# Two transformer blocks on one core: one ScalarE function set with logarithm and exponential, asked for by name ahead of each layer norm

## The reference

```
def layer_norm(x, g, b):
    xf = x.astype(jnp.float32)
    mu = jnp.mean(xf, axis=-1, keepdims=True)
    var = jnp.mean(jnp.square(xf - mu), axis=-1, keepdims=True)
    return ((xf - mu) * lax.rsqrt(var + EPS) * g + b).astype(x.dtype)

for l in range(DEPTH_2):                       # second block, l = 0, 1
    h = x * (1.0 + sc_m) + sh_m
    y = even_mixer(h, ...) if l % 2 == 0 else spatial_gating_mixer(h, ...)
    x = layer_norm_2(ALPHA * x + (1.0 + g_m) * y, ln_g[l, 0], ln_b[l, 0])
    h = x * (1.0 + sc_f) + sh_f
    y = swiglu(h, ...) if l % 2 == 0 else moe_swiglu(h, ...)
    x = layer_norm_2(ALPHA * x + (1.0 + g_f) * y, ln_g[l, 1], ln_b[l, 1])
```

## Time and profile before

| | us |
|---|---|
| median of 3 runs | 2342.64 |
| lowest, highest | 2341.39, 2345.26 |
| the profiled execution, its own time | 2345.24 |
| its span in the trace | 2343.4 |

### The profile page before, as it was taken

How to read it: one execution, slowest core, us unless ns; L and a number is a source line. 1 busy time by engine, 2 the same in 40 slices (tenths; PEclk the granted TensorE clock), 3 DMA queues, 4 the chain that set the end, 5 groups by cost and what they waited for, 6 DMA issues and landing times.

```text
span 2343.4 us, 25110 instructions
## 1 busy us (share of the span) xinstructions
PE 2232.7 (95%) x10088; PEld 1823.9 (78%) x10088; DVE 1600.0 (68%) x1938; ACT 1299.0 (55%) x1569; POOL 17.8 (1%) x16
## 2 busy tenths in 40 slices
PE   8999999997999989799989899999999999999997
PEld 7668877886888866678857788888888888888885
DVE  0266234535999953355422599999999999899994
ACT  1145113105777743344420477787777787778784
POOL 0000000000000000000000000000000000000000
PEclk9999999997999999999999799999999999999998
DMA  8465455755999972045350499999999998999992
GB/s 344 183 254 231 162 202 228 271 214 217 383 367 351 354 285 108 0 180 191 149 217 1 175 392 368 368 362 364 378 352 379 350 381 343 373 352 386 350 371 83
DMA packets 52991, 645.43 MB, mean 275 GB/s; under 512 B 8832, under 2 KB 10624, under 8 KB 14080
## 3 DMA queue, kind: packets, MB, share of 16 engines
q1 hardware_dynamic: 48320, 630.34, 69.6%
q10 hardware_dynamic: 3104, 8.13, 0.9%
q0 software_dynamic: 1440, 5.24, 0.6%
HBM read 640.55 MB, written 3.15 MB: 275 GB/s over the span
## 4 chain that ended last, share of the span: by engine, by line
PE 90%; DVE 4%; ACT 2%; issue 2%; DMA 1%; SPq 0%; ACTq 0%; DVEq 0%
PE psum L1755 56%; PE psum L1545 19%; PE psum L1537 5%; PE psum L1864 2%; DVE stage_lo L1343 1%; PE psum L1639 1%; PE psum L1777 1%; DMA ring<-w_branch_in 1%; PE psum L1650 1%; PE psum L1765 1%; ACT arena L569 1%; DVE h_lo L1440 0%; DMA ring<-w_in_in 0%; PE psum L1567 0%; PE psum L1486 0%
## 5 line engine op out<-in xcount | busy, mean ns | idle before, releaser
L1343 DVE TENSOR_TENSOR stage_lo<-ring,stage_hi 128x1024 fp32r<-128x1024 f32 (+1 forms) x934 | 1103.0, 1217 | 94.5 <-ACT stage_hi L962 77.7
L962 ACT ACTIVATE stage_hi<-ring 128x1024 fp32r<-128x1024 f32 (+1 forms) x934 | 964.4, 1055 | 305.7 <-PE psum L1755 227.4
L1755 PE MATMUL psum<-stage_hi,x_hi 128*128 128x512 f32 (+1 forms) x1344 | 530.2, 395 | 12.8 <-DVE x_lo L1372 8.8
L1755 PE MATMUL psum<-stage_hi,x_lo 128*128 128x512 f32 (+1 forms) x1344 | 522.2, 389 | 0.0
L1755 PE MATMUL psum<-stage_lo,x_hi 128*128 128x512 f32 (+1 forms) x1344 | 520.7, 387 | 0.0
L1755 PEld LDWEIGHTS psum<-stage_hi,x_hi 128*128 128x128 f32 x1344 | 253.2, 188 | 62.2 <-issue 9.1
L1755 PEld LDWEIGHTS psum<-stage_hi,x_lo 128*128 128x128 f32 x1344 | 253.1, 188 | 53.3
L1755 PEld LDWEIGHTS psum<-stage_lo,x_hi 128*128 128x128 f32 x1344 | 253.6, 189 | 49.3
L1755 PE MATMUL psum<-stage_hi,h_hi 128*128 128x512 f32 x664 | 260.1, 392 | 10.0 <-DVE h_lo L1440 9.8
L1755 PE MATMUL psum<-stage_lo,h_hi 128*128 128x512 f32 x664 | 258.5, 389 | 0.0
L1545 PE MATMUL psum<-arena,ring 128*128 128x256 f32 x1024 | 227.1, 382 | 5.6 <-ACT arena L569 3.8
(11 more groups left out here) (218 smaller groups left out, 1685.8 us busy)
## 6 DMA issues: line engine op xcount, KB each, us to landing
ring<-moe_w_gate_in SPq DMA_DIRECT2D x56, 2048.0 KB, 9.3
ring<-moe_w_up_in SPq DMA_DIRECT2D x56, 2048.0 KB, 9.4
ring<-moe_w_down_in SPq DMA_DIRECT2D x56, 2048.0 KB, 9.2
ring<-w_in SPq DMA_DIRECT2D x48, 2048.0 KB, 8.9
ring<-ada_w_in SPq DMA_DIRECT2D x15, 2048.0 KB, 8.0
ring<-w_in_in SPq DMA_DIRECT2D x14, 2048.0 KB, 10.7
mixer_tiles<-ada_w_in SPq DMA_DIRECT2D x9, 2048.0 KB, 7.8
mixer_tiles<-w_in_in SPq DMA_DIRECT2D x6, 2048.0 KB, 12.5
```

Source lines behind the costliest of these rows:

```text
L962: act.activation(chunk_view(stage_hi, f, side, p, c), chunk_source(f, side, p, c), ACT.Copy)\
L1343: dve.tensor_tensor(chunk_view(stage_lo, f, side, p, c), chunk_source(f, side, p, c), chunk_view(stage_hi, f, side, p, c).bitcast(F32), AL ...
L1755: ins = pe.matmul(dst, a, b, start=start, stop=stop)
```

## The change

A function `keep_ln_exp` on ScalarE asks for the set `natural_log_exp_and_others` by name. It is called in five places of ScalarE's program: behind the last Sigmoid of the first mixer, behind the last Gelu of the third mixer, and behind each of the three feed-forward stages. The second of those in the order of the program serves two layer norms, since between numbers 1 and 2 ScalarE uses no other function than Exp, Square, Copy and Identity. The arithmetic stays as written, with Exp now read from this set. Nothing is changed on the other engines.

```
+        def keep_ln_exp():
+
+            act.preload_act_table_set("natural_log_exp_and_others")
...
                         ins = act.activation(gate[:, 2 * i + k, :], bank(b, 2, T)[:, k, :], ACT.Sigmoid,
                                              bias=col_a("b_gate", n * KT + 2 * i + k))
                     ins.then_inc(bank_free[b], 1)
+                    if n == 2 and i == 3:
+                        keep_ln_exp()
...
                     if a == "od_u":
                         act.activation(mix[:, 2 * i:2 * i + 2, :], bank(b, 2, T), ACT.Gelu_apprx_tanh)\
                            .then_inc(bank_free[b], 1)
+                        if i == 3:
+                            keep_ln_exp()
...
             passes(act, n, feeds[n], unit, joined)
+            keep_ln_exp()
         walk(plans[3])
```

## The result

The changed kernel takes 2331.62 us (median of 5 runs, 2330.01 to 2332.82) against 2342.64 before. The ratio of the two is 0.9944 with a 95% interval of 0.9934 to 0.9955: 0.56% faster, where 7.6 us or 0.33% were forecast. The medians differ by 11.0 us, the ratio stands for 13.1. The second is nearer the truth: in the interleaved runs of the experiments the kernel before had medians of 2344.06 to 2345.13, above the 2342.64 of its first runs. Its profiled execution took 2331.94 us with a span of 2330.1.

A forecast was written before the change was run, and what follows sets the result against it. TensorE makes up 90% of the chain of waits, and ScalarE's loads matter only where it waits, in six layer norms. 6 x 1.27 = 7.6 us off 2342.64, all else 0, gave 2335.0 us, range 2331.0 to 2340.0.

The forecast's parts named there:

- The chain and the loads in it: Six layer norms: the load between logarithm and exponential delays TensorE; removing it gains 1.27 us each, 7.6 us (7.3 to 7.9).
- All six pass it on: Behind each layer norm's exponential: the whole gain reaches TensorE; tightest in layer norm 2, with 0.13 us to spare on VectorE.
- The removed load ahead of the logarithm at nothing: Six layer norms: this load runs under TensorE's sum with idle time behind it (2.45 us in number 0), gaining nothing.
- The added loads at nothing: Five earlier loads of 1.28 us on ScalarE: hidden in idle time of at least 6.77 us, costing nothing.
- The transfers behind the added load at 0: Ahead of layer norm 3: four transfers on ScalarE's queue behind the load cost 0, with 4.5 us as upper end.
- The sum: Whole kernel: -7.6 + 0 = -7.6 us, taken from the median of 2342.64 to give 2335.0.
- The forecast's own stretch: Whole kernel: 2332.5 to 2337.5 us around the forecast of 2335.0, given 60%.
- The same clock brings more: Rival on TensorE's clock: two more stretches at full clock give -7.6 - 3.4, 2331.6 us; chance 12%.
- The clock as the other side: Rival: sums of squares fall to half clock, 1.69 us each; 2338 to 2342 (8%), or 2343.5 and above (3%).
- a drain of 1.38 us: Rival at the six loads: a drain hidden in recorded durations goes too, gain 16.0 us, time 2326.6; chance 3%.
- late transfers: Rival ahead of layer norm 3: transfers behind the added load come late, 2339.5 us, or 2337 in half; chance 9%.
- hidden loads: Rival in the layer norms: loads are hidden anyway, or the set doesn't serve both functions; nothing gained, 2342.6 us; chance 5%.

The follow-up runs named there:

- every Copy put back: Changed kernel with a ScalarE Copy of 128x1280 between logarithm and exponential, in all six or some layer norms; in all six 2344.70 us, ratio to before 1.0000.
- Delays in four layer norms: Changed kernel with a ScalarE Copy of 1.27 us between logarithm and exponential in layer norms 0, 2, 4 and 5: 2343.64 us; in 1 and 3 alone: 2338.49.
- two added products in each pause: Changed kernel with two added products (0.9 us at full clock) on TensorE in each pause behind the sum of squares: 2335.14 us, ratio 0.9953.
- the Copy in layer norm 0: Changed kernel with a ScalarE Copy of 1.27 us between logarithm and exponential in layer norm 0 alone: 2336.56 us, ratio to before 0.9965.
- the reverse edit: Changed kernel with a ScalarE Copy of 128x1280 between logarithm and exponential in each layer norm: 2344.70 us, ratio to before 1.0000.

## Why the prediction was right or wrong

*The chain and the loads in it: right.* The load between the two functions was a link; the gap left is 0.03 us where 0.04 was taken, and the pauses are 1.28 us shorter where 1.27 was forecast. Six of them make 7.7 us for 7.6.

*All six pass it on: right.* VectorE in layer norm 2, the tightest place, takes up the exponential at once.

*The removed load ahead of the logarithm at nothing: right,* and shown alone (ratio 1.0002). *The added loads at nothing: right.* All five ran in idle time.

*The transfers behind the added load at 0: right.* All four were issued ahead of it and landed in time.

*The sum: wrong by its missing term.* The step that failed is "The saving is of fixed durations, so it holds for the median too". The sum has no term for TensorE's clock: it was put at nothing, with chances on both sides, since its falls vary. For the sum of squares in layer norm 0 that was so: it went both ways between the pairs of traces. Over the whole kernel it wasn't. With the shorter pauses the time at half clock went from 94 to 77 us on average, for every Copy put back it rose again, and the time moved with it. This term, at 0 in the sum, measured 11.0 - 7.7 = 3.3 us by the medians, 13.1 - 7.7 = 5.4 by the ratio, and 4.7 over all runs of both kernels, where 17 us less at half clock at 0.30 us each make 5.0. In the traces the largest parts are 2.1 us around layer norm 1 and 2.4 in the stages behind layer norms 2 and 4. The forecast's own stretch from 2332.5 to 2337.5 misses the median by 0.9 us, and scaled by the ratio (2342.64 x 0.9944 = 2329.5) the time lies below the range.

*The rivals.* "The same clock brings more" is what came: 2331.6, with the shorter pauses as its reason. It had 12%. So the number of a rival came, and its reason holds in part: two stretches at full clock more were its working, and the time at half clock fell by 17 us in many places. The prediction weighed the clock's two sides nearly alike, 12% against 11%. Every kernel here with longer pauses than the changed one was slower by more than the pauses, and none was slower by less. The clock as the other side, a drain of 1.38 us, late transfers and hidden loads didn't come. The drain would have made the fixed part 16.0 us, and the pauses show 7.7.

*Open.* Why the time at half clock moves as it does. Delays in four layer norms cost 12.2 us and in two 7.0, while all six cost 12 to 13, and the time at half clock doesn't add up either (16 and 10 us more, against 17). More idle time alone doesn't decide it: two added products in each pause left the clock and the time about where they were. And TensorE is busy only 3.8 us less in the mean of the traces; the other 2.2 of the 6.0 us are idle time outside the pauses, which matches waits in and ahead of layer norms 1 and 5 that are 2.4 us shorter in all. Ahead of the sum of layer norm 5 it was 2.32 to 2.77 us in the three traces of before and 1.11 and 1.13 in the changed kernel. TensorE's idle time between the two sums of layer norm 1, behind the branch, was 2.07 us in four of the ten traces and 2.12 to 5.62 in the other six. In the trace of the Copy in layer norm 0:

```profile
863.20 3.69 PE L1650 MATMUL psum<-arena 128*128 128x256 f32 x16 [0.91 <-DVE arena L1169]
872.52 2.90 PE L1650 MATMUL psum<-arena 128*128 128x256 f32 x6 [5.62 <-ACT arena L560]
```

The cause of these waits wasn't tried, nor whether they hang on the clock.

## What to carry to other kernels

Where a short instruction stands alone between two engines' work, a table load there costs its full length each time; asking early for one set that holds both functions moves it under other work for nothing. Look in the timeline for what starts right behind it, and not at ScalarE's busy share. When a stall on TensorE's path is shortened or added and the rows around it show the granted clock falling, expect more than its length (here 1.4 to 1.7 times: 11.0 to 13.1 us for pauses shorter by 7.7). Don't read the excess off one product that got faster: take a stretch wide enough to hold the falls that moved, and compare the granted clock over many runs.

## What the runs showed of the hardware that was not expected

A change of the delay in a chain by 7.7 us moved the time by 11 to 13, and the reverse edit gave it back to within 0.1%. Behind a pause of 2.93 us the granted clock fell at the start of a product and behind 1.64 it didn't, but there a fall of the same 3.4 us had come ahead of the pause, at the same cost. Over the executions of a kernel, 1 us more at half clock went with 0.30 us more of time. ScalarE's queue issued four transfers that stand behind a table load in its order before that load began, while a copy was still running. An exponential that waits by semaphore for the logarithm on the same engine starts 0.03 us behind its end.
